# Attention by pairs of maps with weight units in each step, norm and mask on GpSimd, inputs transposed inside the stream

## What is computed

```python
for l in range(2):
    h = rmsnorm(x, g_mix_pre[l])
    (a_q, a_k, a_v, b_cq, b_ckv, b_kr, c_q, c_k, c_v) = jnp.split(h @ w_in[l], IN_SPLITS, axis=-1)
    o_a = diff_attention(...)   # 4 heads, two softmax maps each, a = p0 - lam * p1
    o_a = rmsnorm(o_a, diff_head_g[l]) * (1.0 - lam_init)
    o_b = mla_attention(qb, kb, v)           # 4 heads of 96
    o_c = swa_attention(...)                 # 8 heads of 64, a window, a sink per head
    x = x + rmsnorm(jnp.concatenate([o_a, o_b, o_c], -1) @ w_out[l], g_mix_post[l])
    x = x + rmsnorm(cross_attention(rmsnorm(x), rmsnorm(mem), w_xq, w_xkv, w_xo), g_x_post[l])
    gate, up = jnp.split(rmsnorm(x, g_ffn_pre[l]) @ w_ffn_in[l], 2, axis=-1)
    x = x + rmsnorm((silu(gate) * up) @ w_ffn_out[l], g_ffn_post[l])
```

## Time and profile before

| | |
|---|---|
| median of 3 runs | 2503.18 us (2499.67 to 2573.14) |
| profiled execution | 2505.91 us, span 2504.1 us |
| PE, DVE, ACT, POOL busy | 89%, 39%, 43%, 63% of the span |
| HBM traffic | 444.6 MB read, 179 GB/s over the span |
| mean granted clock of PE | 0.941 of full speed |
| chain that ended last, by engine | PE 51%, issue 24%, POOL 17%, DVE 6% |
| POOL, the one group of instructions | 654 subtractions, mean 2.42 us |
| ACT, the split of a unit | 654, mean 1.06 us |

### The profile page before, as it was taken

How to read it: one execution, slowest core, us unless ns; L and a number is a source line. 1 busy time by engine, 2 the same in 40 slices (tenths; PEclk the granted TensorE clock), 3 DMA queues, 4 the chain that set the end, 5 groups by cost and what they waited for, 6 DMA issues and landing times.

```text
span 2504.1 us, 31937 instructions
## 1 busy us (share of the span) xinstructions
PE 2222.6 (89%) x10151; PEld 1794.2 (72%) x10151; DVE 968.2 (39%) x1892; ACT 1085.7 (43%) x1556; POOL 1581.9 (63%) x659
## 2 busy tenths in 40 slices
PE   6978889989889899799989898697999799787996
PEld 5767677777667777587777677576877687666875
DVE  5355465643543434333344332684211410434101
ACT  4444355344443553343444344354543444434442
POOL 6524467766334686687867676503888688666875
PEclk9988999999889999899999999898999899888998
DMA  6423467754223677676867665323566466453663
GB/s 201 135 93 117 145 230 249 252 173 143 101 76 130 226 275 257 212 276 237 301 214 248 258 188 154 92 69 109 172 188 202 133 186 202 129 174 113 189 187 107
DMA packets 135700, 447.07 MB, mean 179 GB/s; under 512 B 22506, under 2 KB 28098, under 8 KB 135608
## 3 DMA queue, kind: packets, MB, share of 16 engines
q1 hardware_dynamic: 128920, 426.62, 51.6%
q10 hardware_dynamic: 6688, 19.23, 2.3%
HBM read 444.60 MB, written 3.03 MB: 179 GB/s over the span
## 4 chain that ended last, share of the span: by engine, by line
PE 51%; issue 24%; POOL 17%; DVE 6%; ACT 1%; POOLq 0%; ACTq 0%; DVEq 0%
POOL w_lo L708 17%; PE ps L1623 15%; PE ps L1625 15%; PE ps L1624 15%; PE ps L1953 1%; PE ps L1976 1%; DVE z L1357 1%; PE ps L1723 1%; PE ps L1806 1%; PE ps L1964 1%; DVE z L1354 1%; PE ps L2030 1%; PE ps L1795 0%; DVE h_lo L1180 0%; ACT aff L925 0%
## 5 line engine op out<-in xcount | busy, mean ns | idle before, releaser
L708 POOL TENSOR_TENSOR w_lo<-land,w_hi 128x1024 fp32r<-128x1024 f32 x654 | 1578.2, 2420 | 893.2 <-ACT w_hi L738 891.4
L738 ACT ACTIVATE w_hi<-land 128x1024 fp32r<-128x1024 f32 x654 | 692.2, 1060 | 1029.5 <-PE ps L1625 935.1
L1623 PE MATMUL ps<-w_hi,h_hi 128*128 128x512 f32 (+1 forms) x1872 | 745.1, 398 | 55.4 <-DVE z L1354 16.9
L1625 PE MATMUL ps<-w_hi,h_lo 128*128 128x512 f32 (+1 forms) x1872 | 734.9, 393 | 0.0
L1624 PE MATMUL ps<-w_lo,h_hi 128*128 128x512 f32 (+1 forms) x1872 | 734.5, 392 | 0.0
L1623 PEld LDWEIGHTS ps<-w_hi,h_hi 128*128 128x128 f32 x1872 | 355.6, 190 | 149.0 <-issue 28.3
L1625 PEld LDWEIGHTS ps<-w_hi,h_lo 128*128 128x128 f32 x1872 | 355.4, 190 | 75.6
L1624 PEld LDWEIGHTS ps<-w_lo,h_hi 128*128 128x128 f32 x1872 | 355.9, 190 | 71.1
L1206 DVE TENSOR_TENSOR hid_lo<-ps,hid_hi 128x512 f32 (+1 forms) x77 | 53.2, 691 | 584.6 <-ACT hid_hi L848 584.6
L1623 PE MATMUL ps<-w_hi,hid_hi 128*128 128x512 f32 x616 | 247.6, 402 | 19.6 <-DVE hid_lo L1206 8.6
L1625 PE MATMUL ps<-w_hi,hid_lo 128*128 128x512 f32 x616 | 244.5, 397 | 0.0
(11 more groups left out here) (247 smaller groups left out, 2020.8 us busy)
## 6 DMA issues: line engine op xcount, KB each, us to landing
land<-ffn_w_in_dram SPq DMA_DIRECT2D x220, 512.0 KB, 3.6
ada_land<-ada_w_dram SPq DMA_DIRECT2D x144, 512.0 KB, 5.0
land<-ffn_w_out_dram SPq DMA_DIRECT2D x110, 512.0 KB, 4.1
land<-w_ffn_in_dram SPq DMA_DIRECT2D x88, 512.0 KB, 3.7
land<-w_ffn_out_dram SPq DMA_DIRECT2D x44, 512.0 KB, 4.8
land<-na_w_qkv_dram SPq DMA_DIRECT2D x40, 512.0 KB, 3.5
land<-w_xkv_dram SPq DMA_DIRECT2D x32, 512.0 KB, 3.6
land<-w_in_dram SPq DMA_DIRECT2D x32, 488.0 KB, 3.4
```

Source lines behind the costliest of these rows:

```text
L708: pool.tensor_tensor(w_lo[:, slot, :], land[:, slot, :], w_hi[:, slot, :].bitcast(F32), ALU.subtract).then_inc(*my.up("lo_ready"))
L738: act.activation(w_hi[:, slot, :], land[:, slot, :], ACT.Copy).then_inc(*my.up("hi_ready"))
L1623: pe.matmul(dst, lh, wh, start=first, stop=False)
L1625: done = pe.matmul(dst, ll, wh, start=False, stop=last)
```

## The change

- **Mixer and NA attention by pairs** (`attend` on all engines). A turn i scores pair i, transposes and weighs pair i-1, and holds the units of `KV_IN` (mixer), `V_IN` (NA: the last group of four of `na_w_qkv`, for half of V) and `OUT_IN` (the first units of the output product). DVE handles a pair's outputs in one operation where it can. NA's maps are ordered so that a pair is two heads of the same 128 queries; from pair 4 on two pairs of score banks alternate, and the probabilities have three buffers.
- **Scale factors** are put into q when it is copied, so the maximum comes negated out of the reduction.
- **GpSimd** does the norm of the difference heads (after the second unit of `w_out`) and adds the mask to the bias of each NA head; its loop is cut in pieces for that. Bias tables of six heads are held.
- **NA inputs**: `products_na` does the rope per group out of PSUM and transposes keys and queries inside the stream.
- **FFN outputs** in three places call `make_h` after unit 18 of 22 (`then`). The `taken` of the norms comes in two steps, and the next stage waits for the first.
- The transposes of `o` and the output units are interleaved (`out_unit`), also in NA.

The diff, cut to its core (DVE's and ACT's loops are alike to PE's):

```diff
+THEN_AT = FC - 4
+KV_BANKS = ((6, 7), (0, 2), (0, 2), (0, 2))
+KV_IN = {0: (6, 7), 1: (8,), 2: (9,), 3: (10, 11), 4: (12,), 5: (13,), 6: (14,), 7: (15,)}
+KV_OUT_IN = {1: 1, 4: 2, 8: 3}
+DIFF_SQ_IN = (5, 6)
+V_IN = {0: (0, 1), 1: (2,), 2: (3,)}
+OUT_IN = {"mixer": {9: 0, 10: 1}, "na": {17: 0}}
+TURN_O_IN = {"mixer": {8: (0, 1), 10: (2,)}, "na": {16: (0, 1), 17: (2,)}}
@@ order of the stages
-            do("make_h", "io", mod=(1, 0))
-            do("post_rms", FC)
...
-            do("ffn_out", "ffn_w_out_200", ada=ADA_OUTS)
-            do("make_h", "x", mod=(0, 0))
+            do("ffn_out", "ffn_w_out_200", ada=ADA_OUTS, then=dict(src="x", mod=(0, 0)))
...
-                    do("turn_keys", "qkv", 0, keysT)
-                    do("products", "na_w_qkv", 6, GW, "qkv")
-                    do("turn_keys", "qkv", 0, qT_n)
-                    do("turn_keys", "qkv", D, kT_n)
+                    do("products_na")
+                    ln_rows(0, 0, 5, 1)
                     do("attend", "na", 0)
-                    ln_rows(0, 0, 5, 1)
-                    do("turn_o", "o_n")
-                    do("products_y", "na_w_out")
+                    do("products_y", "na_w_out", done=1)
@@ POOL
+            def diff_norm(l):
+                pool.wait_ge(sems["diff_sq"], my.next("diff_sq", 2))
+                step(pool.tensor_scalar(mean, stat[:, 20:28], 1.0 / DIFF_V, EPS, ALU.mult, ALU.add))
...
+                for _ in range(3):
+                    step(pool.tensor_tensor(part, mean, guess, ALU.mult))
+                    step(pool.tensor_tensor(part, part, guess, ALU.mult))
+                    step(pool.tensor_scalar(part, part, -0.5, 1.5, ALU.mult, ALU.add))
+                    step(pool.tensor_tensor(guess, guess, part, ALU.mult))
...
+                for t in range(T):
+                    step(pool.tensor_tensor(heads[t], heads[t], spread(gain[:, 4 * t:4 * t + 4], DIFF_V, 2), ALU.mult))
+                    ins_ = pool.tensor_tensor(heads[t], heads[t], spread(ghead[:, l, :], DIFF_H), ALU.mult)
+                ins_.then_inc(*my.up("o_done"))
+            def mask(h):
+                pool.tensor_tensor(bias_n(h), bias_n(h), mask_n[:, :, :], ALU.add).then_inc(*my.up("bias_ready"))
@@ DVE, one map of NA
-                        step(dve.scalar_tensor_tensor(s, bias_n[:, h % 4, mp["t"], :], 1.0 / mp["scale"], s, ALU.mult, ALU.add))
-                        step(dve.tensor_tensor(s, s, mask_n[:, mp["t"], :], ALU.add))
-                        step(dve.tensor_reduce(mstat[:, 0, m, 0:1], bank(m % banks), AX, ALU.max))
+                        step(dve.tensor_tensor(s[:, 0:SEQ], bias_n(mp["head"])[:, mp["t"], :], s[:, 0:SEQ], ALU.add))
+                        dve.tensor_reduce(mstat[:, 1, m, 0:1], s, AX, ALU.max, negate=True).then_inc(*my.up("max_ready"))
@@ DVE, the outputs of a pair
+                    step(dve.reciprocal(inv, den))
+                    if one["diff"] is None:
+                        got = ps[:, OUT:OUT + 2, :].rearrange("p c (t s) -> p c t s", t=T)[:, :, 0:w, 0:d]
+                        dve.tensor_tensor(one["both"].rearrange("p t (c d) -> p c t d", c=2), got, spread(inv, d, 3),
+                                          ALU.mult).then_inc(*my.up("o_taken", 2))
+                        return
@@ PE, a turn (waits left out)
+                for i in range(TURNS[which]):
+                    back = weighed_in(which, i)
+                    if 2 * i < len(maps):
...
+                        score_pair(i)
...
+                    if back is not None:
+                        turn_probs(2 * back)
+                        turn_probs(2 * back + 1)
                     if which == "mixer":
...
+                        for u in KV_IN.get(i, ()):
+                            kv_unit(u)
...
+                    for kp in TURN_O_IN[which].get(i, ()):
+                        turn_heads_o(which, kp)
+                    if OUT_IN[which].get(i) == 0:
+                        out_unit(0)
...
+                    if back is not None:
+                        weigh(2 * back)
+                        weigh(2 * back + 1)
@@ ACT, FFN out
+                if then:
+                    split(THEN_AT)
+                    make_h(**then)
+                    split(FC - THEN_AT)
```

More of the change, by code:

```diff
@@ new lines, in mask, with products_na, attend @@
+            def mask(h):
+                slot = f"bias_in{h % NA_BIAS}"
+                pool.wait_ge(sems[slot], my.next(slot, 64))
+                pool.tensor_tensor(bias_n(h), bias_n(h), mask_n[:, :, :], ALU.add).then_inc(*my.up("bias_ready"))
+            def products_na():
+                los(seen[0] + RING)
+                pool.wait_ge(sems["na_in"], my.next("na_in", 32))
+                for h in range(NA_BIAS):
+                    mask(h)
+                units(4 * NA_GROUPS)
+            def attend(which, l):
+                if which == "mixer":
+                    los(seen[0] + 2)
+                    diff_norm(l)
+                elif which == "na":
+                    los(seen[0] + RING)
+                    for h in range(NA_BIAS, NA_H):
+                        mask(h)
@@ L1332, in ffn_out @@
                     ada_columns(columns)
+                if then:
+                    make_h(**then)
+                if columns is not None:
+                    ada_folds(columns)
             def post_rms(units):
@@ L1447, in outputs @@
[L1447 to L1466 removed]
+                    inv = mstat[:, 4, m, :]
@@ new lines, in attend @@
+                if which == "cross":
+                    for m in range(len(maps) + OUT_LAG):
+                        if m < len(maps):
+                            maxima(m)
+                        if m >= OUT_LAG:
+                            outputs(m - OUT_LAG)
+                    return
+                for i in range(TURNS[which] + 1):
+                    back = weighed_in(which, i - 1) if i else None
+                    if back is not None:
+                        output_pair(back)
+                    if which == "mixer" and i in KV_OUT_IN:
+                        kv_out(KV_OUT_IN[i])
+                    if which == "na" and i == V_OUT_IN:
+                        v_out()
+                    if 2 * i < len(maps):
+                        maxima(2 * i)
+                        maxima(2 * i + 1)
+                    for kp in TURN_O_IN[which].get(i, ()):
+                        o_lo(kp)
@@ L1776, in ffn_out @@
                         ada_sum()
-                    if k == FC - 3 and columns is not None:
+                    if k == THEN_AT - 1 and columns is not None:
                         ada_columns(columns)
+                    if k == THEN_AT and then:
+                        make_h(**then)
             def post_rms(units):
```

621 lines of the change are left out of this document (367 added, 254 removed).

## The result

The changed kernel takes 2405.6 us (median of 4 runs, 2400.5 to 2409.7), 0.9616 of the time before, 95% interval 0.9574 to 0.9658: 96 us less, where 128 were forecast. (Two of the four runs of the kernel before, at 2572 and 2573 us, fell in a slower state; the ratio uses the other two, 2499.7 and 2503.2.) The profiled execution took 2409.35 us (span 2407.5), 96.6 less than the profiled one of before.

A forecast was written before the change was run, and what follows sets the result against it. The prediction took the weight stream as PE-bound, 1785 of 2504 us, leaving 719 to the change. Mixer 50, NA 47 and transitions 9.5, 15 and 6.3 sum to 128: 2505.9 - 128 = 2378 us, range 2352 to 2430.

The forecast's parts named there:

- NA's turn: Neighbourhood attention: a turn takes 3.8 us of PE work instead of 4.97; NA as a whole gains 47 us.
- rival A: The chain through DVE and ACT sets the attention pace: mixer 8.8, NA 4.97 us a turn; total 2430; chance 0.20.
- Mixer: Mixer attention, twice: PE sets the pace, 102.5 us a layer against 127.6 and 126.2; gain 50 us.
- `diff_norm` on POOL: Mixer: difference-head norm moved to POOL, small operations 0.4 and 0.85 us, 9.4 in all, 1.3 to 1.5 late.
- rival B: Mixer: small operations on POOL are dear, 1.2 us each, 14.7 late: 2404 us, at the bound 2450; chance 0.08.
- Masks: NA: 16 masks on POOL, about 1.2 us each, six in PE's pause, ten where POOL is idle; 19 if uncovered.
- NA up to its turns: NA before its turns: twenty units 54.6, transposes 5.3, slow restart 1.7, together 61.6 us; rope wait of 17.95 gone.
- Context to latent: Transition from context to latent: 10.8 + 1.9 us becomes 1.8 + 1.8; gain 9.5 us.
- First block to context: Transition from first block to context: squares of the norm stand behind ACT's splits, PE restarts after 4.7 us; gain 6.3.
- Latent FFN: Latent feed-forward stage's `make_h` and the seam at 1475.53: h handled under the last units; gain 15 us together.
- rival D: Handling h inside the stream meets POOL, h_lo 2.8 instead of 0.65, PE 5 us later at three places: 2393; chance 0.10.
- Rival C: Attention turns: the clock stays at 1.2 GHz, so they take twice as long, +228 us: 2606; chance 0.03.

## Where the prediction was wrong, and where right

The step that failed is NA's turn: "a turn is 1.06 + 0.9 + 1.8 = 3.8" compares the work of three engines and leaves out what they wait for from each other. The turn lasts 5.07, and NA gained 30.2 us instead of 47. Two smaller steps failed in the transitions: what stands on DVE ahead of the norm (2.3 for 6.3), and what POOL runs beside after the early restart (10.0 for 15). Of the 31.4 us missing these three are 25.8.

- **Bound, stream, direction**: right. 2405.6 lies within 2352 to 2430, but the likeliest time, 2378, was 28 too low, and the upper end of that range is the price of rival A, which did not come in the mixer: that the time lies within it says little for the sum.
- **Mixer**: right to 1.4 and 2.0 us (103.9 and 104.5 against 102.5). PE sets the pace: turns of 6.6 for the forecast 6.5, no wait over 1.5 us in turns 1 to 7. Rival A's 8.8 did not come. Mis-sized: turn 8, 8.2 for 7.0, with PE at 1.2 GHz behind it, as allowed for.
- **`diff_norm` on POOL**: right. The assumed 0.4 and 0.85 were 0.29 (start to start) and 0.69; it ended at 159.5, before it was asked for, so rival B is out. What the text left out is what it runs beside: its own last multiplication, and a subtraction that it put off, met DVE's small operations. **Masks**: the six before the turns took 1.72 each, the ten in the turns 1.25 to 1.27 (1.2 forecast); PE waited 0.6 us for POOL behind the six, so they are nearly hidden.
- **NA up to its turns**: right (61.6 and 61.6), with the rope inside the groups.
- **NA's turn**: wrong, and this is the largest term. The step "a turn is 1.06 + 0.9 + 1.8 = 3.8" took the longest of three engines' sums (PE 3.8, DVE 3.0, ACT 3.0) and left out the ring of buffers between them. Map m's exponential needs map m-3 transposed, and behind it in ACT's order stand the copies that PE's weighing waits for. Of the 1.27 us a turn 0.73 is this loop (four buffers), 0.25 another wait for the copy that stays, 0.29 PE work taken too small. Ten turns make 12.7; 2.5 are low clock, and the rest lies in the turns around them. In NA rival A's price, 4.97 a turn and 19 us, came nearer, by luck: it is today's PE work for two maps, and not this loop.
- **Context to latent**: right (9.8 for 9.5, restart after 1.3). **First block to context**: the sum has small slips (2.3 + 1.0 + 1.2 is 4.5, not 4.7), which are not what failed. The step that set the squares on ACT as what is late left out nine small operations that the diff puts between `make_h` and the norm on DVE. They held PE for 10.3 us instead of 4.7. With them out of the way the wait is 3.6 and the gain 8.9, more than the 6.3.
- **Latent FFN**: 10.0 for 15. The early restart itself came (1.3). The forecast said POOL is starved while h is handled and drew no line to what follows: POOL then catches up just as the norm's chain of small operations runs, 9.5 us for 2.4, and PE waits 3.5 for POOL's next `w_lo`; the rest of the missing 5 is not traced to a step. This is rival D's cause in another place: the four `h_lo` at each of the three transitions were not caught (0.69 each at most), the root was.
- **Rival C** did not occur in the changed kernel (0.97 to 0.98), but its mechanism did in the one with two buffers: 0.60 and 8.27 us a turn. One buffer less was enough, so it was nearer than its chance of 0.03 says.

## What to carry to other kernels

The turn that three engines share lasted here as long as its longest loop through the buffers, not as the fullest engine. So write down for each buffer what must be done before it is written again, and add the way round, in each engine's order. When a stage restarts earlier, look at what the engines that were at rest now run beside, the tiny operations above all. And measure a removed wait by the length of the whole stretch: one of 6.7 us went here and the stretch stayed as it was.

## What the runs showed of the hardware

- A DVE operation on two or eight elements a row can cost 2.2 to 2.4 us instead of 0.16 when its operands are in SBUF and POOL subtracts 128x1024 beside it; with the intermediate values in PSUM the same chain took 2.4 us instead of 9.5.
- A small POOL operation, 128x8 with a wait for its completion, has a pitch of 0.29 us, one of 128x256 0.69; one of 128x512 (the mask) takes 1.27 alone, and 1.72 in the group of six before NA's turns.
- Waits of 1.4 to 1.7 us in each turn kept TensorE mostly at 1.2 GHz over 82 us (granted clock 0.60); eight idle transposes a turn in those waits brought back 2.4 GHz (1.00) and took 24 us off the kernel. A loop of 5.07 us with a wait of 0.98 ran at the upper clock in most turns: in all ten of one run, in other runs one to four turns fell to the lower.
